# The next phase's first weight unit, multiplied in two halves of the tokens inside the token-major boundary

## The chip, the cores and the metric

The kernel runs on one core of one Trainium2 chip. The metric is the device time in microseconds (us) of one execution; lower is better. Before the change it is 3205.45 us, the median of 3 runs (3203.37 to 3206.9).

## What is computed

Four layers act on a sequence of 512 tokens with 1024 features in float32: an attention layer and a Hyena layer, each followed by a mixture of experts, and then twice a mixing layer with three branches (retention, short convolution, long convolution) and a gated feed-forward layer with a short convolution. Only the second half and the step into it matter here:

```
def second_block(x, ...):                       # x: 1 x 512 x 1024
    for l in range(2):
        h = rmsnorm(x, norm_mix_pre[l])
        proj = h @ w_in[l]                      # 1024 -> 7168
        q, k, v, g_ret, sc_b, sc_c, sc_x, cf_a, cf_b, gate_logits = split(proj)
        y_ret = (silu(g_ret) * head_groupnorm(retention(q, k, v))) @ w_ret_out[l]
        y_sc  = (sc_b * causal_dwconv(sc_c * sc_x)) @ w_sc_out[l]
        y_cf  = silu(layernorm(causal_dwconv(cf_a * sigmoid(cf_b)))) @ w_cf_out[l]
        merged = gates[0] * y_ret + gates[1] * y_sc + gates[2] * y_cf
        x = x + rmsnorm(merged @ w_o[l], norm_mix_post[l])
        h = rmsnorm(x, norm_ffn_pre[l])
        gate, val = split(causal_dwconv(h @ w_up[l], ffn_conv_w[l]))     # 1024 -> 2 x 2816
        x = x + rmsnorm((silu(gate) * val) @ w_down[l], norm_ffn_post[l])
    return x
```

`rmsnorm(x, g)` divides each token by the root of its mean square over the 1024 features and multiplies by `g`. The step from the second mixture of experts into this block is `x = x + g2 * moe(...)`, followed by the same kind of norm.

## The kernel before

**Products.** Every float32 product is made from three products of rounded parts: `split_matmul` (lines 216 to 222) multiplies the weights' low part by the activations' high part, high by high and high by low, into the same sum in PSUM. The weights stream from memory in units of 128 x 2048 numbers (1 MB) through a ring of two places (`Ring`, line 123). For each unit SyncE (queue SP) issues the load, ScalarE (ACT) makes the high part (`make_high`, line 179), and VectorE (DVE, `make_low_beside`, line 349) or GpSimd (POOL, `_make_low`, line 183) makes the low part by subtraction. A load waits until the low part of the unit two before is made, a high part until the products of the unit two before are done (the semaphore `used`), and a product until the low part of its unit is there (`parts`). A unit of 1024 inputs x 256 outputs is 48 matrix products of 128 x 128 weights with 512 tokens.

**Layouts.** Most products put features on the partitions and tokens along the free axis: the weights are the stationary operand and 512 tokens stream past. The last product of a layer is made the other way round: 128 tokens (a tile, there are four, `TT`) are stationary, and the weights stream past, so that a token's 1024 features lie in one partition and its norm is a sum along that partition. PSUM has eight banks of 128 x 512; tile `t` of tokens takes the two banks `2t` and `2t + 1` (`token_psum`).

**The boundary.** At the end of a layer comes the token-major boundary. For each tile `t` of tokens: ACT squares and sums the product and takes a root (`tail_y_root`); DVE inverts it, scales the product by it and by a row of gains, and adds the result to `x` (`residual`, lines 2629 to 2635); ACT squares and sums the new `x` and takes a root (`tail_x_root`); DVE inverts it and scales `x` into `token_h` (`normed`, 2640 and 2641); TensorE (PE) turns the 128 x 1024 tile back by eight transposes into the tile's own two banks (`tail_pe`, 2616); ACT makes the high part of the result (`tail_high`, 2595) and DVE the low part (`low`, 349). There are four such boundaries, of two kinds: from the second mixture of experts into the first mixing phase (gated: no norm of the product, `residual` multiplies by a gate row), and, with the norm, from mixing phase 0 to feed-forward 0, from feed-forward 0 to mixing phase 1, and from mixing phase 1 to feed-forward 1. A fifth, at the very end, only adds the residual and stores the result.

**Order.** Each engine executes its own list of instructions in the order in which the code writes it, and waits where the code says so on semaphores; nothing reorders them. `tail_act`, `tail_pe` and `tail_dve` write the lists of the boundary as a staircase: in step `i` the work on the product of tile `i`, then `normed` and the second root of tile `i - 1`, then the high or low part of tile `i - 2`. All four tiles' transposes stand behind the last product. In step 3 the high and the low part of the next phase's unit 0 are made. Before the boundary the last two units are multiplied tile by tile: `token_units(..., n - 2, 2, t, ...)` makes unit `n - 2` for tile `t`, then unit `n - 1` for it, 12 products each, and signals `y_tile`. A phase is a block of code; between two phases all engines meet at a barrier. In the feed-forward phase POOL makes all low parts, `ring.make_lows(pool, n, False)`; in the mixing phase DVE does. SP's list at the end of a phase is: the loads of this phase, the first two loads of the following phase, then the rows of gains (`norm_rows`, 512 KB each), for which DVE waits at the head of the boundary.

## Time and profile before

| | |
|---|---|
| median of 3 runs | 3205.45 us |
| the profiled execution: its time, its span | 3206.23 us, 3204.5 us |
| PE busy (matrix products) | 2983.5 us, 93% of the span |
| DVE busy | 2023.2 us, 63% |
| ACT busy | 1271.9 us, 40% |
| POOL busy | 356.6 us, 11% |
| mean granted clock of PE | 0.963 of full speed |

The span is the time from the first to the last instruction of one execution that was recorded by the profiler; the run's own time is 1.73 us longer, for what lies around it. A busy share says how much of the span an engine had something in work. A wait is put down to the operation that ended it. The granted clock is 1.00 at 2.4 GHz and 0.50 at 1.2 GHz. Records of matrix products overlap: one lasts from its issue to its modelled end, so the distance between two starts, not the duration, tells what each costs.

### The profile page before, as it was taken

The page shows a single profiled execution, that of the slowest core. Times are in us where ns is not written, and L with a number is a line of the kernel's source. Part 1 is how long each engine was busy: PE and PEld are TensorE (multiplying, and loading weights), DVE is VectorE, ACT ScalarE, POOL GpSimd, SP SyncE. Part 2 cuts the span into 40 slices and gives each one's busy share as a digit, 9 for nine tenths or more (in the row PEclk, how much of TensorE's full clock was granted, in tenths as well). Part 3 has the DMA queues.
Part 4 walks back from the last instruction along what each step waited for, and adds up shares of the span by engine and source line. Part 5 has one row for each costly group of instructions (what it writes and reads, how often), then busy time and mean ns, then how long its engine had stood idle before and what let it go on. Part 6 is the DMA issues. An engine that isn't in the chain of part 4 may idle for free. (4 is left out here: it accounts for less than half of the span.)

```text
span 3204.5 us, 33016 instructions
## 1 busy us (share of the span) xinstructions
PE 2983.5 (93%) x12720; PEld 2342.0 (73%) x12720; DVE 2023.2 (63%) x2443; ACT 1271.9 (40%) x1522; POOL 356.6 (11%) x113
## 2 busy tenths in 40 slices
PE   6898888989899889998999998999989999989998
PEld 5435766768788667777877786888777777778886
DVE  7676699877688559984656645664046665456621
ACT  4542467734211248772222234443232223244422
POOL 0201000000000100000000001444300000024442
PEclk8898899989899989998999998999989999999999
DMA  6144399832200029982222222222322222322222
GB/s 244 61 149 184 142 412 402 323 114 102 69 20 7 30 92 354 356 322 81 92 79 79 92 92 79 92 93 103 106 94 85 78 79 89 109 68 103 92 103 75
DMA packets 91729, 428.39 MB, mean 134 GB/s; under 512 B 10119, under 2 KB 14504, under 8 KB 65225
## 3 DMA queue, kind: packets, MB, share of 16 engines
q1 hardware_dynamic: 88136, 401.36, 34.6%
q10 hardware_dynamic: 3456, 25.17, 2.0%
q8 instruction: 92, 1.51, 0.2%
q14 instruction: 45, 0.36, 0.0%
HBM read 424.39 MB, written 2.10 MB: 133 GB/s over the span
## 5 line engine op out<-in xcount | busy, mean ns | idle before, releaser
L220 PE MATMUL psum<-h_high,weights_low 128*128 128x512 f32 x1856 | 735.7, 396 | 20.8 <-DVE h_low L349 8.3
L221 PE MATMUL psum<-h_high,weights_high 128*128 128x512 f32 x1856 | 730.2, 393 | 0.0
L222 PE MATMUL psum<-h_low,weights_high 128*128 128x512 f32 x1856 | 729.5, 393 | 0.0
L179 ACT ACTIVATE weights_high<-weights_raw 128x2048 fp32r<-128x2048 f32 x166 | 317.8, 1914 | 802.0 <-PE psum L222 767.4
L183 POOL TENSOR_TENSOR weights_low<-weights_raw,weights_high 128x2048 fp32r<-128x2048 f32 x72 | 332.3, 4615 | 2276.8 <-ACT weights_high L179 2276.8
L220 PEld LDWEIGHTS psum<-h_high,weights_low 128*128 128x128 f32 x1856 | 352.9, 190 | 107.3 <-issue 32.0
L349 DVE TENSOR_TENSOR weights_low<-weights_raw,weights_high 128x2048 fp32r<-128x2048 f32 x94 | 215.4, 2292 | 315.8 <-ACT weights_high L179 315.8
L221 PEld LDWEIGHTS psum<-h_high,weights_high 128*128 128x128 f32 x1856 | 352.9, 190 | 75.4 <-issue 1.4
L222 PEld LDWEIGHTS psum<-h_low,weights_high 128*128 128x128 f32 x1856 | 352.6, 190 | 75.6
L1589 DVE TENSOR_TENSOR weights_low<-more_raw,weights_high 128x1024 fp32r<-128x1024 f32 x168 | 203.2, 1221 | 16.6 <-ACT weights_high L1214 10.3
L2752 DVE SCALAR_TENSOR_TENSOR ff_tiles<-psum,params,ff_tiles 128x510 f32<-128x510 f32 (+1 forms) x176 | 123.7, 744 | 135.0 <-ACT ff_tiles L2730 129.0
L1589 DVE TENSOR_TENSOR weights_low<-weights_raw,weights_high 128x1024 fp32r<-128x1024 f32 x168 | 201.4, 1218 | 8.2 <-ACT weights_high L1214 4.3
L1214 ACT ACTIVATE weights_high<-more_raw 128x1024 fp32r<-128x1024 f32 x168 | 178.2, 1061 | 67.3 <-PE psum L1391 34.8
L1389 PE MATMUL psum<-weights_low,slot_x_then_y_high 128*128 128x512 f32 x448 | 184.2, 411 | 13.4 <-DVE weights_low L1589 11.9
L1214 ACT ACTIVATE weights_high<-weights_raw 128x1024 fp32r<-128x1024 f32 x168 | 176.4, 1059 | 38.9 <-PE psum L1391 16.9
L1391 PE MATMUL psum<-weights_high,slot_x_then_y_low 128*128 128x512 f32 x448 | 176.8, 395 | 0.0
L1390 PE MATMUL psum<-weights_high,slot_x_then_y_high 128*128 128x512 f32 x448 | 176.8, 395 | 0.0
L2758 DVE TENSOR_TENSOR ff_tiles<-ff_tiles 128x512 f32<-128x512 f32 x44 | 143.8, 3268 | 30.7 <-ACT ff_tiles L2734 30.7
L2413 DVE SCALAR_TENSOR_TENSOR projections<-long_in,params,projections 128x512 f32<-128x512 f32 x240 | 162.3, 744 | 0.1
L2632 DVE RECIPROCAL token_stats<-token_stats 128x1 f32<-128x1 f32 x16 | 2.6, 164 | 232.5 <-DMA norm_rows<-in_rows 118.0
L220 PE MATMUL psum<-weights_high,ff_low 128*128 128x512 f32 x352 | 139.0, 395 | 7.9 <-POOL weights_low L183 7.9
L221 PE MATMUL psum<-weights_high,ff_high 128*128 128x512 f32 x352 | 138.5, 394 | 0.0
(464 smaller groups left out, 4757.0 us busy)
## 6 DMA issues: line engine op xcount, KB each, us to landing
weights_raw<-in_moe SPq DMA_DIRECT2D x168, 512.0 KB, 5.5
more_raw<-in_moe SPq DMA_DIRECT2D x168, 512.0 KB, 5.5
weights_raw<-in_w_mix SPq DMA_DIRECT2D x76, 1024.0 KB, 4.8
weights_raw<-in_w_ffn SPq DMA_DIRECT2D x66, 1024.0 KB, 4.8
mod_weights<-in_ada_w ACTq DMA_DIRECT2D x24, 1024.0 KB, 8.0
mod_weights<-in_ada_w SPq DMA_DIRECT2D x32, 512.0 KB, 3.6
weights_raw<-in_hy_w_in SPq DMA_DIRECT2D x12, 1024.0 KB, 4.8
mod_weights<-in_ada_w SPq DMA_DIRECT2D x8, 1024.0 KB, 21.9
```

Of the source, the lines that this page charges most:

```text
L179: self.nc.scalar.activation(self.high[:, g % 2, :], self.raw[:, g % 2, :], ACT.Copy).then_inc(self.high_done, 1)
L183: self.nc.gpsimd.tensor_tensor(self.low[:, g % 2, :], self.raw[:, g % 2, :], self.high[:, g % 2, :].bitcast(F32), ALU.subtract).then_inc(s ...
L220: nc.tensor.matmul(out, w[1], rhs[0], start=start, stop=False)
L221: nc.tensor.matmul(out, w[0], rhs[0], start=False, stop=False)
L222: return nc.tensor.matmul(out, w[0], rhs[1], start=False, stop=stop)
L349: return nc.vector.tensor_tensor(low, value, high.bitcast(F32), ALU.subtract)
L1214: nc.scalar.activation(high[v % 4], raw[v % RAWS], ACT.Copy).then_inc(s.high, 1)
L1389: nc.tensor.matmul(out, xh[:, slot, c, :], wl[:, at], start=(c == 0), stop=False)
L1390: nc.tensor.matmul(out, xh[:, slot, c, :], wh[:, at], start=False, stop=False)
L1391: mm = nc.tensor.matmul(out, xl[:, slot, c, :], wh[:, at], start=False, stop=(c == KC - 1))
L1589: tt(low[v % 4], raw[v % RAWS], high[v % 4].bitcast(F32), ALU.subtract).then_inc(s.low, 1)
L2413: stt(ca[:, j, :], GP[:, j, k:k + S], m.param("cf_w", 1, c_cw + 4 * k + j), ca[:, j, :], ALU.mult, ALU.add).then_inc(s.taps, 1)
```

## The change

The four boundaries with a next phase get six edits.

- The next phase's unit 0 is multiplied inside the boundary (`tail_first_unit`), first for tokens 0 to 255, then for tokens 256 to 511. Each half (`first_unit_columns`) is 48 products with 256 tokens streaming, of which 32 need only the high parts of `h` and 16 the low parts. Its results go to banks 0 and 1. The next phase begins at unit 1.
- The transposes of tile 0 and tile 1 move in among the last products (`FLIP_BEHIND`): tile 0 behind unit `n - 2` of tile 2, tile 1 behind unit `n - 2` of tile 3. In the gated boundary they stand behind the products of tile 2 and of tile 3. The transposes of tiles 2 and 3 stand between the two halves of unit 0 (in the gated boundary, tile 2 ahead of the first half and tile 3 between).
- ACT and DVE also make the parts of the next phase's unit 1 in the boundary, and their lists are written out by hand in a new order.
- SP issues the rows of gains ahead of the two loads of the following phase.
- In the feed-forward phases the low part of the last unit, `n - 1`, is made by DVE instead of POOL; in the first of them DVE also waits for the load of the following phase's unit 0.
- In the next phase ACT and DVE no longer make the parts of unit 1.

The diff, without the renumbered calls and the unchanged bodies:

```
 class Ring:
-        if following is not None:
-            for k in range(2):
-                self._load(sp, following[k, :, :])
+        if following is not None:
+            self.stream_following(sp, following)
...
 # phase_moe, scalar: the gated boundary
-                tail_act(nc, act, m, s, post=False, ring=ring)
+                ring.make_high(act, 0)
+                ring.make_high(act, 1)
+                gated_tail_act(nc, act, m, s)
 # phase_moe, tensor
+                flip = tail_flips(nc, pe, m, s)
                 for t in range(2, TT):
                     back_tokens(t, range(SLOTS)).then_inc(s.y_tile, 1)
-                tail_pe(nc, pe, m, s)
+                    flip(t - 2)
+                flip(2)
+                tail_first_unit(nc, pe, ring, 0, m, s, flip, (3,))
 # phase_moe, vector
+                ring.make_low_beside(dve)
+                ring.make_low_beside(dve)
                 dve.wait_ge(s.rows_here, 16)
-                tail_dve(nc, dve, m, s, link, gate_row[:, :], pre_row[:, 0, :], gated=True, ring=ring)
+                tail_dve(nc, dve, m, s, link, gate_row[:, :], pre_row[:, 0, :], gated=True)
...
 # phase_mix, sync
-            ring.stream(sp, d.w_mix[layer], n, following)
+            ring.stream(sp, d.w_mix[layer], n)
             sp.wait_ge(s.here, 16)
             sp.wait_ge(s.merged, 6)
             load_rows(sp, s, norm_rows, (d.rows[4 * layer + 1, :, :], d.rows[4 * layer + 2, :, :]))
+            ring.stream_following(sp, following)
 # phase_mix, tensor
-            for t in range(TT):
-                token_units(pe, ring, MIX_OUT + 2, 2, t, m.Gs, m.psum, MIX_OUT).then_inc(s.y_tile, 1)
+            flip = tail_flips(nc, pe, m, s)
+            last_token_units(pe, ring, MIX_OUT + 2, m.Gs, m.psum, MIX_OUT, s, flip)
             pe.wait_ge(s.y_tile, TT)
             pe.sem_inc(ring.used, 1)
-            tail_pe(nc, pe, m, s)
+            tail_first_unit(nc, pe, ring, n, m, s, flip, (2, 3))
...
+LAST_TILES = [(v, t) for t in range(TT) for v in range(2)]
+FLIP_BEHIND = {(0, 2): 0, (0, 3): 1}
+
+def first_unit_columns(nc, pe, ring, w, m, s, tiles):
+    at = slice(tiles[0] * P, (tiles[-1] + 1) * P)
+    block = lambda part, j, k: part[:, k, j * P:(j + 1) * P]
+    pe.wait_ge(s.t_high, tiles[-1] + 1)
+    for j in range(2):
+        for k in range(KC):
+            nc.tensor.matmul(m.psum[:, j, at], block(w[1], j, k), m.Hh[:, k, at], start=(k == 0), stop=False)
+            nc.tensor.matmul(m.psum[:, j, at], block(w[0], j, k), m.Hh[:, k, at], start=False, stop=False)
+    pe.wait_ge(s.t_ready, tiles[-1] + 1)
+    for j in range(2):
+        for k in range(KC):
+            mm = nc.tensor.matmul(m.psum[:, j, at], block(w[0], j, k), m.Hl[:, k, at], start=False, stop=(k == KC - 1))
+    return mm
+
+def tail_first_unit(nc, pe, ring, u, m, s, flip, between):
+    w = [part.rearrange("p (k m) -> p k m", k=KC) for part in ring.parts(pe, u)]
+    pe.wait_ge(s.t_ready, 1)
+    first_unit_columns(nc, pe, ring, w, m, s, (0, 1))
+    for t in between:
+        flip(t)
+    first_unit_columns(nc, pe, ring, w, m, s, (2, 3)).then_inc(ring.used, 1)
...
 # phase_ffn, gpsimd and vector
-            ring.make_lows(pool, n, False)
+            ring.make_lows(pool, n - 1, False)
...
+            g = ring.first + n
+            dve.wait_ge(ring.low_done, g - 1)
+            if following is not None:
+                dve.wait_ge(ring.loaded[g % 2], 16 * (g // 2 + 1))
+            ring.make_low_beside(dve)
             dve.wait_ge(s.rows_here, 16 if last_layer else 32)
```

How the lists change at the boundary from mixing phase 0 to feed-forward 0. `token_h` is the normed tile on its way to the transposes, `token_stats` holds sums and roots, `h_high` and `h_low` are the parts of the next phase's input.

On PE, before: the last product, all transposes, the branch of the barrier, and then unit 0 of the next phase with 512 tokens.

```order
L222 MATMUL psum<-weights_low,merged_high 128x512
L2616 MATMUL psum<-consts,token_h 128x128 x32
L2160 UNCONDITIONAL_BRANCH
L2698 UNCONDITIONAL_BRANCH
L220 MATMUL psum<-h_high,weights_low 128x512
```

On PE, in the changed kernel, the end of the first half of unit 0 and the start of the second:

```order
L2608 MATMUL psum<-h_high,weights_low 128x256
L2609 MATMUL psum<-h_high,weights_high 128x256
L2613 MATMUL psum<-h_low,weights_high 128x256 x16
L2697 MATMUL psum<-consts,token_h 128x128 x16
L2608 MATMUL psum<-h_high,weights_low 128x256
L2609 MATMUL psum<-h_high,weights_high 128x256
```

Sixteen of the 32 transposes stay behind the products, now between two halves of unit 0; the other sixteen have moved ahead, in two groups of eight.

On ACT, before, from the third tile's product root to the end of the boundary:

```order
L2576 ACTIVATE token_h,token_stats<-psum 128x1024
L2578 ACTIVATE token_stats<-token_stats,consts 128x1
L2585 ACTIVATE token_h,token_stats<-x 128x1024
L2588 ACTIVATE token_stats<-token_stats,consts 128x1
L2595 ACTIVATE h_high<-psum 128x8x128
L2576 ACTIVATE token_h,token_stats<-psum 128x1024
L2578 ACTIVATE token_stats<-token_stats,consts 128x1
L179 ACTIVATE weights_high<-weights_raw 128x2048
```

On ACT, in the changed kernel, from the high part of the next unit 0 to that of unit 1:

```order
L183 ACTIVATE weights_high<-weights_raw 128x2048
L2636 ACTIVATE token_h,token_stats<-psum 128x1024
L2638 ACTIVATE token_stats<-token_stats,consts 128x1
L2655 ACTIVATE h_high<-psum 128x8x128
L2636 ACTIVATE token_h,token_stats<-psum 128x1024
L2638 ACTIVATE token_stats<-token_stats,consts 128x1
L2645 ACTIVATE token_h,token_stats<-x 128x1024
L2648 ACTIVATE token_stats<-token_stats,consts 128x1
L183 ACTIVATE weights_high<-weights_raw 128x2048
```

The high part of unit 0 stood behind the fourth tile's product root and now stands ahead of the third tile's.

On DVE, in the changed kernel, from the low part of the next unit 0 to the end of the boundary:

```order
L353 TENSOR_TENSOR weights_low<-weights_raw,weights_high 128x2048
L2714 RECIPROCAL token_stats<-token_stats 128x1
L2715 SCALAR_TENSOR_TENSOR token_h<-psum,token_stats,norm_rows 128x1024
L2717 TENSOR_TENSOR x<-x,token_h 128x8x128
L353 TENSOR_TENSOR h_low<-psum,h_high 128x8x128
L2714 RECIPROCAL token_stats<-token_stats 128x1
L2715 SCALAR_TENSOR_TENSOR token_h<-psum,token_stats,norm_rows 128x1024
L2717 TENSOR_TENSOR x<-x,token_h 128x8x128
L2722 RECIPROCAL token_stats<-token_stats 128x1
L2723 SCALAR_TENSOR_TENSOR token_h<-x,token_stats,norm_rows 128x1024
L2722 RECIPROCAL token_stats<-token_stats 128x1
L2723 SCALAR_TENSOR_TENSOR token_h<-x,token_stats,norm_rows 128x1024
```

Before, the low part of unit 0 stood behind the fourth tile's residual; it now stands ahead of the third tile's, and `normed` of tiles 2 and 3 follow each other behind the last residual.

## Rows read from the trace of the kernel before

**Rows 1.** The waits of PE: in total, times, the longest.

```profile
PE psum L2616 <- DVE token_h L2641: 33.5, 8, 7.9
...
PE psum L220 <- POOL weights_low L183: 7.9, 2, 3.9
```

**Rows 2.** The timeline of PE, second boundary: start, duration, idle before.

```profile
1928.38 0.50 PE L220 MATMUL psum<-weights_high,merged_low 128*128 128x512 f32 x1 [1.69 <-DVE weights_low L349]
...
1947.86 1.94 PE L2616 MATMUL psum<-consts,token_h 128*128 128x128 f32 x16
1957.75 1.97 PE L2616 MATMUL psum<-consts,token_h 128*128 128x128 f32 x8 [7.94 <-DVE token_h L2641]
...
1964.88 0.77 PE L220 MATMUL psum<-h_high,weights_low 128*128 128x512 f32 x1 [2.64 <-PEq L2160]
```

**Rows 3.** PE in windows, second boundary: length, busy (records), granted clock.

```profile
1926.00:1928.00 2.00, 0.69 (x4) 1.00 0.00 0
1952.00:1954.00 2.00, 0.00 (x0) 0.54 0.00 0
1968.00:1970.00 2.00, 2.00 (x8) 0.69 0.69 291
```

**Rows 4.** The timeline of DVE, second boundary.

```profile
1935.65 0.17 DVE L2632 RECIPROCAL token_stats<-token_stats 128x1 f32<-128x1 f32 x1 [7.32 <-DMA norm_rows<-in_rows]
...
1937.17 1.23 DVE L2635 TENSOR_TENSOR x<-x,token_h 128x1024 f32<-128x1024 f32 x1
...
1954.02 2.28 DVE L349 TENSOR_TENSOR weights_low<-weights_raw,weights_high 128x2048 fp32r<-128x2048 f32 x1
...
1956.41 1.28 DVE L2641 SCALAR_TENSOR_TENSOR token_h<-x,token_stats,norm_rows 128x1024 f32<-128x1024 f32 x1
...
1963.34 1.22 DVE L349 TENSOR_TENSOR h_low<-psum,h_high 128x1024 fp32r<-128x1024 f32 x1 [1.30 <-ACT h_high L2595]
```

**Rows 5.** The timeline of ACT, second boundary.

```profile
1949.89 1.02 ACT L2576 ACTIVATE token_h<-psum 128x1024 f32<-128x1024 f32 x1
...
1951.23 1.89 ACT L179 ACTIVATE weights_high<-weights_raw 128x2048 fp32r<-128x2048 f32 x1
...
1978.31 1.28 ACT L2730 ACT_TABLE_LOAD   x1 [11.48 <-PE psum L222]
```

**Rows 6.** Products with 256 columns: the timeline of PE, and a line of groups.

```profile
857.22 1.30 PE L1931 MATMUL psum<-weights_high,filter_hidden_first 128*128 128x256 f32 x8
...
858.35 0.40 PE L1935 MATMUL psum<-weights_high,filter_hidden_high 128*128 128x512 f32 x1
...
L1947 PE MATMUL psum<-z_token_major,dft_fwd 128*128 128x256 f32 x256 | 59.8, 393 | 1.1 <-ACT z_token_major L1998 1.1
```

**Rows 7.** The timelines of PE and of ACT, first boundary.

```profile
1466.71 1.91 PE L2616 MATMUL psum<-consts,token_h 128*128 128x128 f32 x16
...
1496.71 1.92 ACT L179 ACTIVATE weights_high<-weights_raw 128x2048 fp32r<-128x2048 f32 x1 [11.54 <-PE psum L222]
...
1507.59 1.92 ACT L179 ACTIVATE weights_high<-weights_raw 128x2048 fp32r<-128x2048 f32 x1 [6.62 <-PE psum L222]
```

**Rows 8.** A line of groups of the page: the low part of a unit on POOL.

```profile
L183 POOL TENSOR_TENSOR weights_low<-weights_raw,weights_high 128x2048 fp32r<-128x2048 f32 x72 | 332.3, 4615 | 2276.8 <-ACT weights_high L179 2276.8
```

**Rows 9.** DMA issues, the page, and 1483 to 1500 us: KB each, us to landing.

```profile
weights_raw<-in_w_ffn SPq DMA_DIRECT2D x66, 1024.0 KB, 4.8
...
weights_raw<-in_w_mix SPq DMA_DIRECT2D x2, 1024.0 KB, 7.7
```

**Rows 10.** The last unit of both feed-forward phases, PE and ACT.

```profile
2311.15 0.79 PE L220 MATMUL psum<-weights_high,ff_low 128*128 128x512 f32 x1 [3.93 <-POOL weights_low L183]
...
2315.52 1.03 ACT L2576 ACTIVATE token_h<-psum 128x1024 f32<-128x1024 f32 x1 [9.01 <-PE psum L222]
...
3174.97 0.79 PE L220 MATMUL psum<-weights_high,ff_low 128*128 128x512 f32 x1 [3.93 <-POOL weights_low L183]
...
3180.49 1.03 ACT L2576 ACTIVATE token_h<-psum 128x1024 f32<-128x1024 f32 x1 [10.16 <-PE psum L222]
```

More of the change, by code:

```diff
@@ L169, in stream, with stream_following @@
         if following is not None:
-            for k in range(2):
-                self._load(sp, following[k, :, :])
+            self.stream_following(sp, following)
+    def stream_following(self, sp, following):
+        for k in range(2):
+            self._load(sp, following[k, :, :])
     def make_high(self, act, u, turn=0, per=4):
@@ L238, in unit_products, with streamed_products @@
     mm.then_inc(ring.used, 1)
-def streamed_products(nc, pe, ring, n, rhs, psum, read_out, k_ready=None, after=None):
-    for u in range(min(n, TURN)):
+def streamed_products(nc, pe, ring, n, rhs, psum, read_out, k_ready=None, after=None, first=0):
+    for u in range(first, min(n, TURN)):
         unit_products(nc, pe, ring, u, rhs, psum, k_ready=k_ready if u == 0 else None)
@@ L2550, in token_psum, with token_units @@
     return m.psum[:, 2 * t:2 * t + 2, :].rearrange("p b n -> p (b n)")
-def token_units(pe, ring, u, n, t, x, psum, first):
-    for v in range(u, u + n):
-        w = [part.rearrange("p (k m) -> p k m", k=2) for part in ring.parts(pe, v)]
-        for half in range(2):
-            for k in range(2):
-                c = 2 * (v - first) + k
-                mm = split_matmul(ring.nc, psum[:, 2 * t + half, :], [part[:, c, t * P:(t + 1) * P] for part in x],
-                                  [part[:, k, half * S:(half + 1) * S] for part in w], c == 0, c == x[0].shape[1] - 1)
-        if n == 2 and v == u and t == TT - 1:
-            mm.then_inc(ring.used, 1)
-    return mm
+def token_units(pe, ring, u, t, x, psum, first):
+    w = [part.rearrange("p (k m) -> p k m", k=2) for part in ring.parts(pe, u)]
+    for half in range(2):
+        mm = token_half(ring, w, 2 * (u - first), t, half, x, psum)
+    return mm
@@ new lines, in token_half, with last_token_units @@
+def token_half(ring, w, c0, t, half, x, psum):
+    for k in range(2):
+        c = c0 + k
+        mm = split_matmul(ring.nc, psum[:, 2 * t + half, :], [part[:, c, t * P:(t + 1) * P] for part in x],
+                          [part[:, k, half * S:(half + 1) * S] for part in w], c == 0, c == x[0].shape[1] - 1)
+    return mm
+LAST_TILES = [(v, t) for t in range(TT) for v in range(2)]
+FLIP_BEHIND = {(0, 2): 0, (0, 3): 1}
+def last_token_units(pe, ring, u, x, psum, first, s, flip=None):
+    w = {}
+    for v, t in LAST_TILES:
+        if v not in w:
+            w[v] = [part.rearrange("p (k m) -> p k m", k=2) for part in ring.parts(pe, u + v)]
+        for half in range(2):
+            mm = token_half(ring, w[v], 2 * (u + v - first), t, half, x, psum)
+        if (v, t) == (0, TT - 1):
+            mm.then_inc(ring.used, 1)
+        if v == 1:
+            mm.then_inc(s.y_tile, 1)
+        if flip is not None and (v, t) in FLIP_BEHIND:
+            flip(FLIP_BEHIND[v, t])
@@ L2617, in tail_pe @@
         mm.then_inc(s.h_flip, 1)
+    return flip
 def tail_dve(nc, dve, m, s, link, row, pre=None, gated=False, keep=True, ring=None):
@@ L2648, in low @@
         low_part(nc, m.Hl[:, :, at], by_feature(token_psum(m, t)), m.Hh[:, :, at]).then_inc(s.t_ready, 1)
-    for step in range(TT + 2):
-        if step < TT:
-            residual(step)
-        if ring is not None and step == TT - 1:
-            ring.make_low_beside(dve)
-        if pre is not None and 1 <= step <= TT:
-            normed(step - 1)
-        if pre is not None and step >= 2:
-            low(step - 2)
+    if pre is None:
+        for t in range(TT):
+            residual(t)
+    elif gated:
+        residual(0)
+        residual(1)
+        normed(0)
+        normed(1)
+        residual(2)
+        low(0)
+        normed(2)
+        residual(3)
+        low(1)
+        normed(3)
+        low(2)
+        low(3)
+    else:
+        residual(0)
+        normed(0)
+        residual(1)
+        low(0)
+        normed(1)
+        ring.make_low_beside(dve)
+        residual(2)
+        low(1)
+        residual(3)
+        normed(2)
+        normed(3)
+        low(2)
+        low(3)
+        ring.make_low_beside(dve)
 def phase_ffn(nc, m, ph, ring, d, layer, following):
@@ L2713, in _ @@
             if not last_layer:
[L2714 removed]
+                tail_first_unit(nc, pe, ring, n, m, s, flip, (2, 3))
         def tap(u, turn, j, k):
```

66 lines of the change are left out of this document (41 added, 25 removed).

## The prediction

> **What bounds the kernel now.** I read the waits of PE first. PE is busy 93% of the span, so time can only come from its idle stretches, from a low clock, or from less work. Its largest wait in the second half is for the normed tile `token_h`: 33.5 us in 8 waits, two in each boundary, and two more are for the low part of a feed-forward unit, 3.9 us each [rows 1]. Then I read the timeline of PE at the second boundary [rows 2]. The last products end at about 1947.7, sixteen transposes follow in 1.94 us, then PE is idle 7.94 us, turns tile 2, waits 0.56, turns tile 3, and starts unit 0 at 1964.88 after 2.64 us of barrier. Unit 0 is done when ACT can read it, 1978.2 [rows 5]. So 30.5 us lie between the last product and the end of unit 0, of which 10.9 are unit 0's own work at full clock: two units end 10.88 us apart [rows 7], 48 products at 0.227.
>
> Third, the clock in windows. It fell to 0.50 about 2.4 us into the idle time and came back only at about 1969.2, 4.3 us after unit 0 had begun, though a pause of 1.69 us at 1926.7 left it at 1.00 [rows 3, 2]. Eight transposes take 1.97 us there and sixteen took 1.94 before the fall: twice the price [rows 2]. Unit 0 pays 2.2 us for its start.
>
> Fourth, what PE waits for. At the head DVE waits for the gain rows until 1935.65 [rows 4], although the first root was ready at 1934.15 (tile 0's product at 1931.4, square 1.03, reading the sum 0.2, a table load of 1.28, root 0.3). From there DVE works nearly without a pause to 1964.56. DVE and ACT, then, not PE, set the length of the boundary, and there is work PE could do beside them.
>
> **The changed second boundary, step by step.** Durations: `residual` 2.75 (1935.65 to 1938.40), `normed` 1.45, low part of a tile 1.22, of a unit 2.28 (used as 2.2 where the next one follows) [rows 4]; square and root 1.35 (1949.89 to 1951.23), high part of a unit 1.89, of a tile 1.0 like the square over the same 128 x 1024 [rows 5]; a transposition of a tile 0.97 at full clock, 1.97 at half [rows 2]. A tile of products is 24 x 0.227 = 5.44, half of it 2.72.
> - Tile 0's product is there at 1931.40. The rows of gains now stand ahead of the loads and are long there, so `residual` 0 runs 1934.2 to 1936.95, ACT's root to 1938.45, `normed` 0 to 1939.95. PE finishes (unit n-2, tile 2) at 1939.45, waits 0.5, transposes until 1940.95, and goes on: tile 2's product is ready at 1943.7, (n-2, tile 3) at 1946.4.
> - Tile 1: `residual` to 1942.65, low part of tile 0, `normed` 1 to 1945.65. No wait for its transposes: 1947.35. The last product is ready at 1950.1, against 1947.7 before. Moving two flips costs 2.4 here, but 1.94 of it was behind the products.
> - ACT now stands at the high part of the next unit 0, which waits for `used` of unit n-2 until 1946.4, done 1948.3. Queued behind it is tile 2's product root, ready to start since 1943.7; it ends 1949.65. DVE makes the unit's low part to 1950.6, `residual` 2 to 1953.3, low part of tile 1 to 1954.4, `residual` 3 to 1957.05, `normed` 2 to 1958.5, `normed` 3 to 1960.1.
> - PE starts the first half of unit 0 at 1950.65 (high part of tile 1 and the unit's low part). What does a product with 256 tokens and new weights cost? The trace has two such kinds [rows 6]: eight from 857.22 to 858.35, 0.141 each, whose operands are rounded parts as here; and 256 that take 59.8 us, 0.234 each, whose operands are plain float32. I take 0.141, because the operands are of the same kind, and keep 0.234 for the range. 48 x 0.141 = 6.8: until 1957.4. Low part of tile 1 at 1954.4 is in time for product 33.
> - Transposes of tile 2 wait for 1958.5, done 1959.45; of tile 3 for 1960.1, done 1961.05; high part 1962.1; the low part at 1963.35 is in time. Second half 1962.1 to 1968.9. The low part of unit 1 ends at 1965.6, beside it. Barrier 2.64: unit 1 starts at 1971.5, where before it started at 1978.2. **Gain 6.7**, though PE does 96 x 0.141 = 13.5 in place of 10.9.
>
> The Trainium skill (TensorE: Matmul & The Clock Gate, section Back-to-back issue gap) gives N/2.4 + 2.5 ns, by which a 256-token product would take 109 ns and a half 5.2 us; as an estimate by that page each boundary would gain 1.6 more in its second half. The row measures 141 ns with new weights for each product, so the measurement decides here.
>
> **What is late next.** In the old order unit 2's load and high part had a unit's time after the barrier; now PE needs unit 2 after unit 1. In a feed-forward phase: load issued 0.4 after the phase start, landed 4.8 later [rows 9], high part 1.9, low part on POOL 4.6 [rows 8]: 11.7, against unit 1's end at 10.9 + 0.05. Cost 0.9. In a mixing phase two tables of 0.5 and 1 MB are issued ahead; the two loads there landed 7.7 us after issue [rows 9], the first some 8.1, issued at 1.3: 9.4, high part 1.9, then DVE's low part 2.3 (and ACT's table load and sigmoid as long): 13.65. Cost 2.75. If the unit starts at half clock, this wait is hidden under the loss.
>
> **The other boundaries.** The third and fourth are like the second (30.4 us on average over the three from last product to end of unit 0). The first is gated, without product roots. The last product is ready at 1466.7, one flip later in the new order: 1467.7. Flips of tiles 1 and 2 end at 1469.6, first half 1469.7 to 1476.45, flip 3 (its `normed` ends 1473.2) 1477.4, high part 1478.5, second half 1485.25, barrier 1487.9; unit 1 started at 1496.7 before [rows 7]. Gain 8.8. The two units' parts stand ahead of the tail, where DVE and ACT are idle.
>
> **The last low part of the feed-forward phases.** POOL needs 4.6, DVE 2.3; PE now waits 3.93 for it [rows 1, 10] and would wait 1.7, as at 1928.38 in the mixing phase where DVE makes it [rows 2]: 2.2 gained in each. The longer wait also let the clock fall. From 2311.15 tile 0 took 4.35 instead of 2.72, 1.6 lost; from 3174.97 it took 5.5, 2.8 lost, and 0.3 in the tile after [rows 10]. The 1.69 us pause cost none. So 3.9 and 5.3. DVE's new wait for the following load adds nothing: SP may issue it when POOL has made the low part of unit n-2, about 6 us ahead of the high part of unit n-1, and a load lands in 4.8. Were it later, each us would be one more of PE's wait. Behind that wait on DVE only the boundary is queued.
>
> **Sum.** First 8.8 - 2.75 = 6.05; second 6.7 - 0.9 = 5.8; third 6.7 - 2.75 + 3.9 = 7.85; fourth 5.8; end 5.3. Together 30.8. From this I take 3.2 for the clock, two losses of the 1.6 seen: around 1957.4 to 1962.1 PE is idle 2.85 of 4.7 us, in three pieces, and at the barrier 2.64. 27.6 remain. The profiled execution took 3206.23 (span 3204.5 and 1.73 around it), 0.8 above the median, which is inside the spread of the runs (3.5). 3206.2 - 27.6 = 3178.6 on its scale, 3178 on the median's. Its own range, with the clock full (3175) or falling more often and unit 2 a little earlier or later, is 3170 to 3186.
>
> **Rivals.**
> - The clock falls between the halves. For it: idle 2.85 of 4.7 us; against: none of the pieces is longer than 1.1, and 1.69 did no harm. Then two flips cost 2.0 more and the second half 2.2 (as unit 0 today), and the restart about 1: 5.1 in each of three boundaries, 15.4. Gain 15.4, 3190. The Trainium skill (same page, section HAM oscillation) says that PE working in bursts between waits starts again at the low clock after them. By the rows 2 and 3, that held for 7.94 us of idling and not for 1.69.
> - The short products cost 0.234. A half is 11.2. Second boundary: 1950.65, 1961.85, flips 1963.75, high part 1964.8, 1976.0, 1978.65: 0.45 lost, and the wait. The first loses 2.85 with its wait, second and fourth 1.35 each, third gains 0.7, the end 5.3. Sum 0.5 gained: 3205, no change. For it: 256 records of that shape. Against: other operand kind.
> - Slower: the clock stays at 0.50 through every boundary, because short products and flips do not bring it back, as the transposes of 1957 to 1962 did not. A half is then 48 x 0.28 = 13.5. Second boundary: 1964.15, flips 1968.1, high 1969.15, 1982.6, start 1985.25 and 2.2 lost by unit 1: 9.2 worse than now. Four times about 9, less 3.9 and 5.3: 27 slower, 3232. It decides from 7.7 lost against my schedule in each boundary. Against: the first half begins right behind the products, at full clock, with no pause over 0.6.
> - The extra preparation in the boundary or unit 2 is later than I have it, by 2 or 3 us each: gain 18, 3187.
>
> **From this the numbers.** Forecast 0.70, clock between the halves 0.12, preparation later 0.07, price 0.234 0.06, slower 0.05. About 0.2% (6.4 us) is what a measurement of this kernel can tell from no change. Faster by more: 0.70 + 0.12 + 0.07 = 0.89. Within: 0.06. Slower: 0.05. The range goes from 3170 to 3196, which takes in the first and the fourth rival and leaves out about 0.15.
>
> **What would show it.** Distance of starts of the 256-token products 0.14; the first half starting within 1 us of the last product and the last high part of the boundary about 14.4 us behind the last product of before; clock 1.00 between the halves; unit 1 starting 23.8 us behind where the last product was; waits of PE for unit 2 of 2.7 in mixing and about 1 in feed-forward phases; waits of 1.7 instead of 3.93 for the last low part. It is wrong if the products cost over 0.2, if the clock reads 0.50 inside the boundaries, or if PE waits for something that I have called hidden.

## The result, and the profile after

The changed kernel takes 3172.49 us, the median of 4 runs (3169.15 to 3179.04), against 3204.41 us of the kernel before on the same chips (4 runs, 3200.91 to 3206.9). The ratio is 0.9904, 95% interval 0.9885 to 0.9922: 31 us faster, 25 to 37. It was forecast at 3178 with 3170 to 3196. A second group of runs gave 3173.32 us and 0.9904 (0.989 to 0.9919).

The profiled execution took 3172.14 us, its span 3170.0, against 3204.5. Not all runs start this part of the program at the same time: the first product of the gated boundary is 1.4 us later than in the profile of before, and over all the kernels below it lies between 1434 and 1443 us, whatever was changed behind it. So I also compare the part from that product to the end of the span, which holds all the edits: 1763.2 us before, 1727.2 after, 36.0 less, which lies inside the 25 to 37 of the ratio.

The waits of PE after (in total, times, the longest), to be held against [rows 1]:

```profile
PE psum L2697 <- DVE token_h L2723: 8.6, 9, 1.8
...
PE psum L224 <- DVE weights_low L353: 6.9, 4, 1.8
...
PE psum L224 <- ACT projections L2364: 5.9, 2, 3.2
...
PE psum L2608 <- ACT h_high L2655: 4.8, 5, 1.1
...
PE psum L2608 <- DVE weights_low L353: 2.4, 3, 0.8
...
PE psum L224 <- POOL weights_low L187: 1.3, 2, 0.7
```

The 33.5 us for the normed tile have become 8.6. The 7.9 us for POOL's last low parts are gone (the POOL row here is a new one, unit 2 in the feed-forward phases); in their place stands DVE with 6.9 in four waits, the 1.7 of the two mixing phases and of the two feed-forward phases. New are 5.9 us for `projections`, an output of ACT, at unit 2 of the mixing phases.

The timeline of PE at the second boundary, the counterpart of [rows 2]:

```profile
1921.02 0.50 PE L224 MATMUL psum<-weights_high,merged_low 128*128 128x512 f32 x1 [1.70 <-DVE weights_low L353]
...
1932.73 1.09 PE L2697 MATMUL psum<-consts,token_h 128*128 128x128 f32 x8 [0.52 <-DVE token_h L2723]
...
1943.71 0.38 PE L2608 MATMUL psum<-h_high,weights_low 128*128 128x256 f32 x1 [0.79 <-DVE weights_low L353]
...
1951.53 1.09 PE L2697 MATMUL psum<-consts,token_h 128*128 128x128 f32 x8 [1.81 <-DVE token_h L2723]
1953.17 1.09 PE L2697 MATMUL psum<-consts,token_h 128*128 128x128 f32 x8 [0.54 <-DVE token_h L2723]
1955.37 0.39 PE L2608 MATMUL psum<-h_high,weights_low 128*128 128x256 f32 x1 [1.11 <-ACT h_high L2655]
...
1955.84 0.28 PE L2609 MATMUL psum<-h_high,weights_high 128*128 128x256 f32 x1
1955.95 0.28 PE L2608 MATMUL psum<-h_high,weights_low 128*128 128x256 f32 x1
...
1961.71 0.47 PE L224 MATMUL psum<-h_high,weights_low 128*128 128x512 f32 x1 [0.32 <-PEq L2171]
...
1973.50 0.50 PE L224 MATMUL psum<-h_high,weights_low 128*128 128x512 f32 x1 [0.62 <-POOL weights_low L187]
```

These rows show that PE, idle 7.94 us here before, now has no pause over 1.81 in this boundary; that the 256-token products start 0.12 us apart (1955.84, 1955.95), so that each half of unit 0 takes 5.9 us; and that the idle time at the barrier, ahead of unit 1, is 0.32 us where it was 2.64.

DVE there, the counterpart of [rows 4]:

```profile
1926.91 0.16 DVE L2714 RECIPROCAL token_stats<-token_stats 128x1 f32<-128x1 f32 x1 [5.95 <-ACT token_stats L2638]
...
1941.36 2.29 DVE L353 TENSOR_TENSOR weights_low<-weights_raw,weights_high 128x2048 fp32r<-128x2048 f32 x1 [3.00 <-ACT weights_high L183]
...
1956.49 2.28 DVE L353 TENSOR_TENSOR weights_low<-weights_raw,weights_high 128x2048 fp32r<-128x2048 f32 x1
```

It no longer waits for the rows of gains (the releaser at 1926.91 is ACT's root). But it stands idle 3.00 us ahead of unit 0's low part, and from there on works without a pause of note to the end.

The clock in windows (length, PE's busy time with its records, granted clock, DMA): inside the second boundary, then in the third, and, below, at unit 2 of the first mixing phase.

```profile
1952.00:1954.00 2.00, 1.46 (x14) 1.00 0.00 0
...
2326.00:2328.00 2.00, 1.82 (x8) 0.54 0.00 0
2330.00:2332.00 2.00, 2.00 (x11) 0.50 0.03 8
1500.00:1502.00 2.00, 2.00 (x5) 0.53 0.50 94
```

In the second boundary of before, [rows 3] has 1.00 ahead of the idle time, 0.54 from 1952 and 0.69 at 1968; between them, from 1956 to 1968, it is 0.50. After, the clock stays at 1.00 in the first, second and fourth boundary and falls in the third, between the halves, until some 2333. It falls once more at 1500, behind the wait for unit 2.

That wait, PE first and then ACT, who ends it (the counterparts of [rows 7] and [rows 5]):

```profile
1499.98 0.63 PE L224 MATMUL psum<-h_high,weights_low 128*128 128x512 f32 x1 [3.21 <-ACT projections L2364]
```

```profile
1495.60 1.91 ACT L183 ACTIVATE weights_high<-weights_raw 128x2048 fp32r<-128x2048 f32 x1 [16.38 <-DMA weights_raw<-in_w_mix]
...
1498.82 1.02 ACT L2364 ACTIVATE projections<-psum 128x1024 f32<-128x1024 f32 x1
```

```profile
weights_raw<-in_w_mix SPq DMA_DIRECT2D x2, 1024.0 KB, 9.5
```

ACT idles 16.38 us until the load of unit 2 has landed, then makes its high part, loads a table and makes the sigmoid that PE awaits.

The last unit of the feed-forward phases, against [rows 10]:

```profile
2293.84 0.50 PE L224 MATMUL psum<-weights_high,ff_low 128*128 128x512 f32 x1 [1.77 <-DVE weights_low L353]
...
3143.31 0.50 PE L224 MATMUL psum<-weights_high,ff_low 128*128 128x512 f32 x1 [1.75 <-DVE weights_low L353]
```

```profile
3146.36 1.03 ACT L2636 ACTIVATE token_h<-psum 128x1024 f32<-128x1024 f32 x1 [5.50 <-PE psum L226]
```

The wait is 1.77 and 1.75 in place of 3.93, and tile 0 is done 3.05 us after the restart (3143.31 to 3146.36), not 5.5.

**Where the 36 us came from.** Shifts of like events between the two traces: first boundary, to the start of unit 3, 7.1 us; second 7.8; the last low part of feed-forward 0 3.5; third boundary 3.9; fourth 6.9; the last low part and tail of feed-forward 1 5.1. That is 34.3. The other 1.7 appear in the first mixing phase, where nothing was changed, and the traces show where: behind eight products with a contraction of only 4 rows (1700.34 before, 1694.68 after) the clock falls in both, and stays low for about 6.8 us before and 3.4 after. Some 8 us behind the start of these products, before and then after:

```profile
1708.00:1710.00 2.00, 2.00 (x6) 0.54 0.51 213
```

```profile
1702.00:1704.00 2.00, 2.00 (x10) 1.00 0.65 274
```

The length of this fall varies from profile to profile: in the second mixing phase it is the second profile of the changed kernel, below, that loses 1.6 us more than the first. Whether the change has a hand in the 1.7 us is not shown. In the first mixing phase the long fall stands in the three profiles of the kernel before and its variants and in that with unit 0 in one piece, the shorter one in both profiles of the changed kernel.

### The profile page after: what moved, and what is told of

Same layout as the page of the kernel before. It is cut to its first block and busy times, and to the rows that moved or that the text cites. A ratio compares the mean times of both kernels' runs of the same rounds, so it can differ in the third digit from the quotient of the medians.

```text
span 3170.0 us, 33394 instructions
## 1 busy us (share of the span) xinstructions
PE 2974.9 (94%) x12912; PEld 2341.8 (74%) x12912; DVE 2031.5 (64%) x2447; ACT 1272.4 (40%) x1522; POOL 338.4 (11%) x109
## 5 line engine op out<-in xcount | busy, mean ns | idle before, releaser
L224 PE MATMUL psum<-h_high,weights_low 128*128 128x512 f32 x1792 | 707.7, 395 | 18.8 <-DVE h_low L353 8.3
L225 PE MATMUL psum<-h_high,weights_high 128*128 128x512 f32 x1792 | 702.5, 392 | 0.0
L226 PE MATMUL psum<-h_low,weights_high 128*128 128x512 f32 x1792 | 702.1, 392 | 0.0
L187 POOL TENSOR_TENSOR weights_low<-weights_raw,weights_high 128x2048 fp32r<-128x2048 f32 x68 | 314.1, 4620 | 2240.8 <-ACT weights_high L183 2240.8
L353 DVE TENSOR_TENSOR weights_low<-weights_raw,weights_high 128x2048 fp32r<-128x2048 f32 x98 | 224.5, 2292 | 497.2 <-ACT weights_high L183 497.2
L224 PEld LDWEIGHTS psum<-h_high,weights_low 128*128 128x128 f32 x1792 | 338.8, 189 | 102.0 <-issue 21.3
L225 PEld LDWEIGHTS psum<-h_high,weights_high 128*128 128x128 f32 x1792 | 338.8, 189 | 72.5 <-issue 1.4
L226 PEld LDWEIGHTS psum<-h_low,weights_high 128*128 128x128 f32 x1792 | 338.8, 189 | 72.5
L226 PE MATMUL psum<-weights_low,ff_high 128*128 128x512 f32 x352 | 137.0, 389 | 0.0
## 6 DMA issues: line engine op xcount, KB each, us to landing
mod_weights<-in_ada_w SPq DMA_DIRECT2D x8, 1024.0 KB, 21.7
```

Source lines behind the costliest of these rows:

```text
L187: self.nc.gpsimd.tensor_tensor(self.low[:, g % 2, :], self.raw[:, g % 2, :], self.high[:, g % 2, :].bitcast(F32), ALU.subtract).then_inc(s ...
L224: nc.tensor.matmul(out, w[1], rhs[0], start=start, stop=False)
L225: nc.tensor.matmul(out, w[0], rhs[0], start=False, stop=False)
L226: return nc.tensor.matmul(out, w[0], rhs[1], start=False, stop=stop)
L353: return nc.vector.tensor_tensor(low, value, high.bitcast(F32), ALU.subtract)
```

## The experiments

Eight kernels, in two groups; each group shares its runs of the kernel before (3203.37 and 3205.49 us). "Part" is the time from the first product of the gated boundary to the end of the span, in the profiled execution; two profiles of the same changed kernel gave 1727.2 and 1730.9, so differences under 4 us in it are not told apart, except where the trace shows them in place. The 3.7 us between these two profiles are stretches at the low clock: the second has 1.3 us more in feed-forward 0, 1.6 in the second mixing phase and 1.5 in the fourth boundary, and 0.7 less around the third. One of them is at the last unit of feed-forward 0 in the second profile, PE and then its clock:

```profile
2291.21 0.50 PE L224 MATMUL psum<-weights_high,ff_low 128*128 128x512 f32 x1 [1.77 <-DVE weights_low L353]
```

```profile
2294.00:2296.00 2.00, 2.00 (x6) 0.50 0.59 250
```

Behind the same wait of 1.77 us the clock stayed at 1.00 in the first profile.

| | median us | ratio to before (95%) | part us |
|---|---|---|---|
| before | | | 1763.2 |
| whole change, again | 3173.32 | 0.9904 (0.9890 to 0.9919) | 1730.9 |
| low part by VectorE only | 3193.68 | 0.9973 (0.9963 to 0.9984) | 1754.6 |
| rows first only | 3201.86 | 1.0000 (0.9991 to 1.0008) | 1763.1 |
| unit 0 in one piece | 3189.46 | 0.9960 (0.9946 to 0.9975) | 1749.5 |
| third load early | 3151.97 | 0.9841 (0.9825 to 0.9856) | 1715.7 |
| product root first | 3157.41 | 0.9855 (0.9838 to 0.9872) | 1720.7 |
| both | 3146.26 | 0.9818 (0.9804 to 0.9833) | 1708.9 |
| both, flip between passes | 3144.80 | 0.9814 (0.9800 to 0.9827) | 1704.8 |

### The whole change, again

No edit; it stands beside the others of its group.

> The changed kernel as it is, beside the others of this group. Expected 3172 us, about 32 below the kernel before, as its first runs gave (3169 to 3179).

Measured: 3173.32 us, 0.9904, as expected.

### One part alone: the last low part by VectorE

```
 # the kernel before, phase_ffn
-            ring.make_lows(pool, n, False)
+            ring.make_lows(pool, n - 1, False)
...
+            g = ring.first + n
+            dve.wait_ge(ring.low_done, g - 1)
+            if following is not None:
+                dve.wait_ge(ring.loaded[g % 2], 16 * (g // 2 + 1))
+            ring.make_low_beside(dve)
             dve.wait_ge(s.rows_here, 16 if last_layer else 32)
```

> The kernel before with one part of the change: in both feed-forward phases VectorE in place of GpSimd makes the low part of the last unit. Theory A (this part is worth what the two traces show at these two places, and nothing of it depends on the boundary): the wait of 3.93 us becomes 1.75 in both phases, the clock does not fall there, 3.5 + 5.0 = 8.5 us gained, so 3196. Rival (the boundary behind it swallows the gain in the first feed-forward phase, since VectorE then waits for the rows of gains, which are issued later than this low part): tiles end earlier but the start of the next unit 0 does not move, only the last phase gains, 5.0, so 3199.5.

Measured: ratio 0.9973, which is 8.7 us, and 8.6 in the part. The waits of PE:

```profile
PE psum L220 <- DVE weights_low L349: 6.9, 4, 1.8
```

POOL's row is gone, and the boundary behind it passes the gain on: unit 0 of the second mixing phase starts 904.1 us behind the first product of the gated boundary, against 907.7 before, so 3.5 arrive there, and 5.1 more by the end. Theory A holds. The rival's 5 us would be a ratio of 0.9984, the very edge of the interval; the place of unit 0 rules it out.

### One part alone: the rows of gains first

```
 # the kernel before, phase_mix; phase_ffn likewise
-            ring.stream(sp, d.w_mix[layer], n, following)
+            ring.stream(sp, d.w_mix[layer], n)
             ...
             load_rows(sp, s, norm_rows, ...)
+            ring.stream_following(sp, following)
```

> The kernel before with one part of the change: the rows of gains are issued ahead of the two loads of the following phase. Theory A (the 1.5 us by which VectorE starts earlier at the head of three boundaries are swallowed by its own pause before the third tile, and the end of the boundary is set from the last product on): 0 us, 3204.4. Rival (the start of the boundary sets its end): three times 1.5, so 3200.

Measured: ratio 1.0000 (0.9991 to 1.0008), and the part is the same to 0.1 us. DVE at the head of the second boundary:

```profile
1926.88 0.16 DVE L2637 RECIPROCAL token_stats<-token_stats 128x1 f32<-128x1 f32 x1 [5.95 <-ACT token_stats L2583]
...
1930.97 0.16 DVE L2637 RECIPROCAL token_stats<-token_stats 128x1 f32<-128x1 f32 x1 [1.35 <-ACT token_stats L2583]
...
1936.41 0.16 DVE L2637 RECIPROCAL token_stats<-token_stats 128x1 f32<-128x1 f32 x1 [1.31 <-ACT token_stats L2583]
```

DVE is released at the head by ACT's root, no longer by the DMA of [rows 4], and now pauses 1.35 us ahead of tile 1, where it had no pause before: what it gained at the head it gives back waiting for products. The 1.31 ahead of tile 2 it had before as well. Theory A; the rival's 4.5 us would be a ratio of 0.9986, outside the interval. The wait at the head of the chain was worth nothing, since the chain is paced further on.

### Undone: unit 0 in one piece

```
 # the changed kernel, tail_first_unit
-    first_unit_columns(nc, pe, ring, w, m, s, (0, 1))
     for t in between:
         flip(t)
-    first_unit_columns(nc, pe, ring, w, m, s, (2, 3)).then_inc(ring.used, 1)
+    first_unit_columns(nc, pe, ring, w, m, s, (0, 1, 2, 3)).then_inc(ring.used, 1)
```

> The changed kernel with unit 0 still inside the boundary and all other parts of the change, but multiplied once for all 512 tokens behind the last transposes, not in two halves. Theory A (the gain of the boundary is that the first half fills PE's idle time while VectorE works on tiles 2 and 3, which also holds the clock): PE is idle 8 us again, the clock falls to 0.50, and unit 0 costs 10.9 + 2.2 us behind the last high part where the second half cost 5.9: 7 us later in each of three boundaries and about 4 in the gated one, 25 in all, so about 3197. Rival (the gain comes from the order of the lists, the earlier transposes and unit 1's parts made ahead): no more than 5 us in all, so 3173 to 3178.

Measured: 3189.46, 16 us above the whole change; the part 19 to 22 above it. PE, and its clock, at the second boundary:

```profile
1948.12 3.65 PE L2696 MATMUL psum<-consts,token_h 128*128 128x128 f32 x16 [8.70 <-DVE token_h L2722]
1952.88 0.50 PE L2608 MATMUL psum<-h_high,weights_low 128*128 128x512 f32 x1 [1.11 <-ACT h_high L2654]
...
1964.39 0.47 PE L224 MATMUL psum<-h_high,weights_low 128*128 128x512 f32 x1 [0.32 <-PEq L2171]
```

```profile
1946.00:1948.00 2.00, 0.00 (x0) 0.50 0.00 0
...
1950.00:1952.00 2.00, 1.76 (x9) 0.50 0.00 0
1952.00:1954.00 2.00, 1.12 (x5) 0.98 0.00 0
```

PE is idle 8.70 us again, and unit 1 starts 25 us behind the last product instead of 19 (1942.5 to 1961.71 in the changed kernel). So the halves are the larger part of what the change brings in the boundaries, and the rival (5 us) falls. Unit 1 starts 5.6, 6.2, 3.5 and 5.8 us later behind the last product in the four boundaries, 21 in all. The expected 25 were too many by the clock, on both sides. Here it fell in the idle time, but the sixteen transposes, 3.65 us without a break and begun at 1.2 GHz, were all that PE did before it was back at 2.4 GHz, ahead of unit 0: they paid, 1.7 us, not unit 0. And in the third boundary the changed kernel's own clock had fallen, so less was lost there (3.5).

What is left without the halves is 13.7 us in the part, of which the low parts are 8.6. The other 5 or so are what the earlier transposes, unit 0 ahead of the barrier, unit 1's parts and the order bring, less the new waits for unit 2 (2.15, 1.21 and 2.83 us in the first three phases). No run separates them.

### Undone: the new wait for unit 2

```
 # the changed kernel, phase_mix, phase_ffn and the gated boundary of phase_moe
-    def stream_following(self, sp, following):
+    def stream_following(self, sp, following, count=2):
-        for k in range(2):
+        for k in range(count):
...
-            ring.stream_following(sp, following)
+            ring.stream_following(sp, following, 3)
...
 # phase_moe, ahead of the gated boundary
-                ring.stream(sp, None, 0, following)
+                ring.stream_following(sp, following, 2 if pre is None else 3)
```

> The changed kernel, and SyncE issues a third load of the following phase (unit 2's) still inside the boundary, as soon as unit 0's low part is made, instead of behind the phase's start. Theory A (PE's new waits for unit 2 of 3.2, 2.7 and twice 0.65 us come from the load's start, and the clock that fell after the longest cost 1.7 more): all four waits go, 9 us gained against the changed kernel, 3164. Rival (in the mixing phases ScalarE's table load and sigmoid, not the load, are late, or the early load collides with others): the waits stay over 2 us in the mixing phases, gain 1 to 2, 3171.

Measured: ratio 0.9841 against 0.9904, part 11.5 to 15 less. No wait for `projections` and none for POOL's low part is left in its list. ACT at the start of the first mixing phase:

```profile
1485.31 1.92 ACT L183 ACTIVATE weights_high<-weights_raw 128x2048 fp32r<-128x2048 f32 x1 [6.44 <-PEq L1106]
...
1488.54 1.03 ACT L2364 ACTIVATE projections<-psum 128x1024 f32<-128x1024 f32 x1
1496.53 1.92 ACT L183 ACTIVATE weights_high<-weights_raw 128x2048 fp32r<-128x2048 f32 x1 [6.97 <-PE psum L226]
```

The high part of unit 2 follows the barrier at once, and the sigmoid is made beside unit 1: theory A. The rival (table load and sigmoid late) falls, although it was ACT's output that PE was seen to wait for: what ended the wait was the last of a chain whose head, the load, was late. The ratio says 13 to 27 us, more than the 9 expected; the part, with less noise, 11.5 against the first profile. From unit 1 to unit 3 the four phases gain 5.0, 1.0, 3.0 and 1.0 us on that profile, 10 in all, of which 9 are the waits and the fallen clock behind the longest; 2.5 more is the fall of the clock in the third boundary, which did not occur in this profile (its second boundary lost 0.9 instead).

### The order of the lists: product root first

```
 # tail_act
-    ring.make_high(act, u)
     tail_y_root(nc, act, m, s, 2)
+    ring.make_high(act, u)
     tail_high(nc, act, m, s, 1)
-    tail_y_root(nc, act, m, s, 3)
     tail_x_root(nc, act, m, s, 2)
+    tail_y_root(nc, act, m, s, 3)
 # tail_dve
-        ring.make_low_beside(dve)
         residual(2)
+        ring.make_low_beside(dve)
```

> The changed kernel with one other order in the three boundaries with a norm: ScalarE takes tile 2's product root ahead of unit 0's high part (which waits for the products of tile 3), and VectorE makes tile 2's residual ahead of unit 0's low part. Theory A (VectorE's list sets the length of the boundary from unit 0's parts on, and stands idle 3.0 us ahead of unit 0's low part): that idle time is filled with the residual, the second half starts 2.8 us earlier in each, 8 us in all, 3165. Rival (PE's own work, products, two halves and transposes, sets it by now): under 2 us in all, 3172.

Measured: 0.9855 against 0.9904, part 6.5 to 10 less. DVE in it:

```profile
1931.59 1.28 DVE L2715 SCALAR_TENSOR_TENSOR token_h<-psum,token_stats,norm_rows 128x1024 f32<-128x1024 f32 x1
...
1934.48 2.29 DVE L353 TENSOR_TENSOR weights_low<-weights_raw,weights_high 128x2048 fp32r<-128x2048 f32 x1 [0.35 <-ACT weights_high L183]
```

The pause ahead of unit 0's low part is 0.35 in place of 3.00. Unit 1 starts 16.8 us behind the last product in each of the three boundaries, against 19.2 in the second and fourth before this edit: 2.4 each where I expected 2.8. Theory A. In the third it is 4.9 (21.7 before the edit), of which 2.5 is the fall of the clock, absent here. The whole change's lists were profiled three times (twice as they are, once with the third load early), nine boundaries with a norm, and the clock fell inside four of them; with this order, in this profile and the two below, it fell inside none of nine.

### Both, and a flip between the passes

> Both of the above. Theory A: the two add, 9 + 8 = 17 us below the changed kernel, 3156. Rival: an earlier phase start shows a new wait for unit 2 or for its low part, so they add to 10 or 12, 3162.

Measured: 3146.26 us, ratio 0.9818, which is 27 us below the changed kernel by the times and 18.3 by the part (22.0 against its second profile). Each alone had 11.5 and 6.5 in the part, together 18.0: the two add, and the rival's 10 to 12 falls, since no new wait for unit 2 appears. PE at the second boundary:

```profile
1931.15 0.39 PE L2608 MATMUL psum<-h_high,weights_low 128*128 128x256 f32 x1 [0.79 <-DVE weights_low L353]
...
1938.23 1.09 PE L2697 MATMUL psum<-consts,token_h 128*128 128x128 f32 x8 [0.19 <-DVE token_h L2723]
1940.44 0.39 PE L2608 MATMUL psum<-h_high,weights_low 128*128 128x256 f32 x1 [1.11 <-ACT h_high L2655]
...
1946.77 0.47 PE L224 MATMUL psum<-h_high,weights_low 128*128 128x512 f32 x1 [0.32 <-PEq L2171]
```

From the last product to unit 1 it is 16.8 us in all four boundaries, and each next unit follows after 11.0 and 10.9. The only waits left inside the second to fourth are 0.53 for tile 0, 0.79 for unit 0's low part, 0.2 for tile 3 and 1.11 for its high part.

```
 # gated boundary: tile 3's transposes between the passes of the first half
     (32 products with the high parts of h, tiles 0 and 1)
+    flip(3)
     (16 products with the low parts)
-    flip(3)
```

> Both of the above, and in the gated boundary tile 3's transposes stand between the high and the low passes of unit 0's first half, so that ScalarE's high part of tile 3 (1.0 us, for which PE waits 1.1) lies beside 16 products. Theory A: 1.1 us less in one place, seen in the trace, not in the time, 3155. Rival (tile 3 is not normed by then): PE waits ahead of the transposes instead, 0 us.

Measured: 3144.80 us, 0.9814, not told apart from 0.9818. In the list of waits the row of the high part went from five waits with 4.8 us to this:

```profile
PE psum L2608 <- ACT h_high L2657: 3.7, 4, 1.1
```

One of 1.1 us is gone, and behind it unit 1 starts 15.4 us behind the last product of the gated boundary in place of 16.8: theory A. The part is 4.1 us less than without this edit; the rest of that is low clock that this profile has less of, 1.6 in the first mixing phase and 1.2 in feed-forward 0. This is the fastest version of the study, 60 us below the kernel before, of which the change brought 31.

## Why the prediction was right, and where not

**The kind of gain: right.** DVE's and ACT's lists set the length of a boundary, and the halves filled PE's idle time beside them; undoing the halves alone cost 16 to 22 us.

**The sum.** Ahead of the 3.2 for the clock, the forecast had 6.05, 5.8, 3.95 and 5.8 us for the four boundaries; measured were 7.1, 7.8, 3.9 and 6.9. For the last low parts it had 9.2, measured 8.6, and 1.7 came from a place that it did not have. So the part lost 36.0 us where 27.6 were forecast. The near hit is in part luck: the errors told below partly cancel, the barrier and the short product on the one side, the clock and the later second half on the other.

**The step of the barrier: mis-sized.** I took the 2.64 us ahead of unit 0 for a barrier that would stand behind the second half as well. After, it is 0.32. [rows 4] had it: tile 3's low part starts at 1963.34 and ends at 1964.56, 0.32 before 1964.88. The rest of the 2.64 was tile 3's high and low part, which I had already put ahead of and beside the second half. I counted them twice, 2.3 us in each of four boundaries, 9.2 in all. This is the largest error of the sum, and the main reason why the time came out below the forecast. Unit 1 starts 21.4 us behind where the last product was in the second boundary, not 23.8.

**The price of a short product: right row, a little high.** 0.12 in place of 0.141, so each half took 5.9 us and not 6.8. The eight of [rows 6] had the right number in them: their first start is 0.31 ahead of the second, the other distances are 0.12, and the mean over all eight took the first in. The row of 0.234 was for another kind of operand. By the formula in the Trainium skill (TensorE: Matmul & The Clock Gate, section Back-to-back issue gap) it is, as an estimate, 0.109; the Trainium skill gives the formula there for a single product, without a budget for the weight load. The trace has 0.12 with new weights for each.

**The order of the lists: right within 0.6 us.** Second half at 14.4 us behind the old place of the last product, by my schedule; measured 15.0 (12.84 behind the last product's start, so 12.5 behind its end, which the two flips had moved by 2.56). The wait for tile 2 is 1.81 where I had 1.1, since the first half was done 0.9 sooner.

**Unit 2: right.** Costs of 2.75 and 0.9; measured 3.21, 0.62, 2.71 and 0.68. What I left open was whether the wait hides a slow clock; instead, in the first mixing phase it made one: unit 2 took 12.6 us instead of 10.9.

**The clock: near in size, 3.2 taken off, but not where I had it.** Measured 2.5 in the third boundary and 1.7 behind the wait for unit 2, 4.2 in all, and none in the second and fourth boundary. By my own signs, a clock of 0.50 inside the boundaries would be wrong, and the third showed it (2330 to 2332): there the rival came true, once in three times in this profile, twice in three in the second one. The argument against it, that a pause of 1.69 us did no harm, rested on one place: behind the wait of 1.77 us in feed-forward 0 the clock fell in two of the eight profiles that have it, the second of the changed kernel and that of both edits together, where it cost 1.6 us.

**The last low part: right.** 3.9 and 5.3 forecast; 3.5 and 5.1 in the trace, 8.7 when alone. That the clock held behind the new wait of 1.77 was chance in part, as just said.

**Rows of gains: as the schedule had it.** Worth nothing alone.

What stays open: why the clock falls behind the 4-row products for 3.4 us in one profile and 6.8 in another, and why the last four kernels came out 8 to 12 us below the times expected for them, which is more than their traces explain. The start of this part moves by some 9 us between profiles of kernels that are the same up to there, and the runs of one kernel spread as much: the five of the third early load lie at 3151 (three) and at 3160 (two), and the profiled one, at 3160, had the late start, 1442. Whether the others started sooner was not recorded.

## What to carry to other kernels

When an idle stretch of the matrix engine is paced by another engine, look for work of the next phase that needs only a part of the data, and split it along the axis on which the data arrives. Then move what the next phase prepares with it, one step further than the work itself: here the load of unit 2 had to move too. Before a gap is called a barrier, subtract what other engines finish inside it; and before a wait at the head of a chain is removed, look whether the chain pauses further on.

## What the runs showed of the hardware

- A 256-column product with new weights each time costs 0.12 us at 2.4 GHz, though its weight load is recorded with 0.19; a 512-column one 0.227. Splitting a unit in two halves cost PE 0.9 us in all: two halves of 5.9 in place of 10.9.
- The clock came back while PE did nothing but transposes: in the kernel with unit 0 in one piece, sixteen without a break (3.65 us) went ahead of a window at 0.98. Eight, a pause of 0.56 and eight more had no such effect in the second boundary of the kernel before, and had it in the fourth, where the window from 2826 reads 1.00; 2.64 us of idle time later, from 2830, it read 0.50 again.
- Waits of nearly one length do not cost one price. Of the 36 waits of 1.69 to 1.77 us for the low part of a last unit in the ten profiles, the clock stayed at 1.00 behind 34 and fell behind 2. For unit 2 it fell behind a wait of 2.05 and one of 2.70, and not behind 2.15 and 2.71; behind those of 2.83 us and more it always fell. So a single harmless pause in a trace does not show that the next of its length is harmless.
- PE can be busy all the time and the clock still fall. In the second mixing phase of the changed kernel, behind eight products whose contraction has only 4 rows:

```profile
2544.06 3.69 PE L2274 MATMUL psum<-root,consts 4*128 4x512 f32 x8
```

```profile
2546.00:2548.00 2.00, 2.00 (x6) 1.00 0.00 0
2548.00:2550.00 2.00, 2.00 (x6) 0.51 0.45 61
2550.00:2552.00 2.00, 2.00 (x7) 0.64 0.75 315
```

The busy time is full in all three windows, and the granted clock goes from 1.00 to 0.51. The same fall stands in both mixing phases of the kernel before, but not with one length: from the profile of before to that after, it is the 1.7 us of the first mixing phase. That the few rows of these products are the cause is a guess; no run here tried it.
